# Depthwise convolution in two half-width PSUM accumulators, and sample value products regrouped, in a conformer and attention trunk on one core

## What is computed

```
z = u @ w_in                      # 2048 -> 3 x 2048
a, b, gate = split(z)
c = a * sigmoid(b)
full = concat([history, c])       # 30 earlier positions
y = depthwise_conv(full, conv_w)  # 31 taps per feature
y = silu(layer_norm(y + conv_b))
out = (y * silu(gate)) @ w_out
```

## Time and profile before

| | |
|---|---|
| Median of 3 runs | 3295.57 us (3295.47 to 3299.87) |
| The profiled execution, own time | 3296.47 us |
| Its span | 3294.8 us |
| TensorE busy | 3107.7 us, 94% |
| VectorE busy | 1503.7 us, 46% |
| GpSimd busy | 1551.4 us, 47% |
| ScalarE busy | 850.9 us, 26% |
| Mean granted TensorE clock | 0.972 of full speed |

### The profile page before, as it was taken

How to read it: one execution, slowest core, us unless ns; L and a number is a source line. 1 busy time by engine, 2 the same in 40 slices (tenths; PEclk the granted TensorE clock), 3 DMA queues, 4 the chain that set the end, 5 groups by cost and what they waited for, 6 DMA issues and landing times.

```text
span 3294.8 us, 50429 instructions
## 1 busy us (share of the span) xinstructions
PE 3107.7 (94%) x19117; PEld 2987.6 (91%) x19117; DVE 1503.7 (46%) x1729; ACT 850.9 (26%) x1708; POOL 1551.4 (47%) x1153
## 2 busy tenths in 40 slices
PE   6999999999999999999968999999999999899996
PEld 6999999999889999999948898899899889799995
DVE  6999999999831114000091324333433343500043
ACT  5121211211221224121231223222222222422232
POOL 2778778787733334333343333233233323144475
PEclk9999999999999999999989999999999999899998
DMA  5121221211122225221272211111111211433386
GB/s 162 41 71 50 57 59 47 71 53 53 55 99 92 89 94 168 65 72 65 85 278 94 57 51 46 51 49 43 55 42 51 55 41 48 142 98 93 98 293 225
DMA packets 171678, 284.87 MB, mean 86 GB/s; under 512 B 62009, under 2 KB 72505, under 8 KB 171577
## 3 DMA queue, kind: packets, MB, share of 16 engines
q1 hardware_dynamic: 127328, 222.48, 22.4%
q10 hardware_dynamic: 41912, 52.32, 4.4%
q0 software_dynamic: 2352, 8.88, 0.7%
HBM read 218.44 MB, written 67.15 MB: 87 GB/s over the span
## 4 chain that ended last, share of the span: by engine, by line
PE 47%; POOL 16%; issue 15%; DVE 13%; ACT 4%; DMA 4%; SPq 0%; POOLq 0%; ACTq 0%; DVEq 0%
PE z_even L514 8%; PE z_even L515 8%; PE z_even L517 8%; PE z_odd L514 7%; PE z_odd L515 7%; PE z_odd L517 6%; POOL w_lo L1017 6%; POOL work L1098 3%; POOL work L1090 3%; DMA work<-conv_scratch 2%; ACT work L935 1%; DVE work L1410 1%; DVE work L1413 1%; POOL work L1126 1%; DMA work<-out_scratch 1%
## 5 line engine op out<-in xcount | busy, mean ns | idle before, releaser
L1017 POOL TENSOR_TENSOR w_lo<-w_raw,w_hi 128x512 fp32r<-128x512 f32 x528 | 748.4, 1426 | 1368.6 <-ACT w_hi L734 1368.0
L514 PE MATMUL z_even<-u_hi,w_hi 128*128 128x364 f32 (+1 forms) x2784 | 926.3, 333 | 79.8 <-POOL u_lo L1178 33.6
L514 PE MATMUL z_odd<-u_hi,w_hi 128*128 128x364 f32 (+1 forms) x2784 | 940.8, 338 | 53.5 <-POOL w_lo L1017 53.5
L515 PE MATMUL z_odd<-u_lo,w_hi 128*128 128x364 f32 (+1 forms) x2784 | 925.3, 332 | 0.0
L515 PE MATMUL z_even<-u_lo,w_hi 128*128 128x364 f32 (+1 forms) x2784 | 922.1, 331 | 0.0
L734 ACT ACTIVATE w_hi<-w_raw 128x512 fp32r<-128x512 f32 x528 | 331.5, 630 | 1690.0 <-PE z_even L517 813.8
L517 PE MATMUL z_odd<-u_hi,w_lo 128*128 128x364 f32 (+1 forms) x2784 | 637.8, 330 | 0.0
L517 PE MATMUL z_even<-u_hi,w_lo 128*128 128x364 f32 (+1 forms) x2784 | 635.2, 329 | 0.0
L514 PEld LDWEIGHTS z_even<-u_hi,w_hi 128*128 128x128 f32 x2784 | 530.4, 191 | 98.6 <-issue 27.0
L514 PEld LDWEIGHTS z_odd<-u_hi,w_hi 128*128 128x128 f32 x2784 | 532.8, 191 | 91.9 <-POOL w_lo L1017 49.7
L515 PEld LDWEIGHTS z_odd<-u_lo,w_hi 128*128 128x128 f32 x2784 | 533.7, 192 | 0.1
(11 more groups left out here) (148 smaller groups left out, 2234.6 us busy)
## 6 DMA issues: line engine op xcount, KB each, us to landing
w_raw<-in_w SPq DMA_DIRECT2D x528, 256.0 KB, 2.7
work<-in_x SPq DMA_DIRECT2D x32, 544.0 KB, 5.8
work<-branch_scratch SPq DMA_DIRECT2D x31, 544.0 KB, 5.1
conv_scratch<-work ACTq DMA_DIRECT2D x16, 544.0 KB, 2.7
work<-conv_scratch SPq DMA_DIRECT2D x16, 544.0 KB, 3.8
resid_scratch<-work ACTq DMA_DIRECT2D x16, 544.0 KB, 6.5
branch_scratch<-work ACTq DMA_DIRECT2D x16, 512.0 KB, 2.6
branch_scratch<-work POOLq DMA_DIRECT2D x15, 544.0 KB, 3.0
```

Source lines behind the costliest of these rows:

```text
L514: pe.matmul(o, w_hi[:, q, at:at + P], chunk(u_hi[:, k, :], c), start=(i == 0), stop=False)
L515: pe.matmul(o, w_hi[:, q, at:at + P], chunk(u_lo[:, k, :], c), start=False, stop=False)
L1017: pool.tensor_tensor(w_lo[:, q, :], w_raw[:, q, :], w_hi[:, q, :].bitcast(F32), ALU.subtract).then_inc(w_lo_ready, 1)
```

## The change

The convolution works in two halves of 512 positions, one in each bank of `aux`. For each half VectorE makes tap 0 with the bias itself, by a `tensor_scalar` from `cp` into PSUM, and then taps 1 to 30, the halves in turn; all accumulate in PSUM. Each of them still waits for the instruction two before it, which is now the same half's tap before. ScalarE's tap 0, the row `odd_taps`, the semaphore `tap0_ready` and the final addition are gone. The last taps count up `conv_ready` by two for each group. VectorE may start the next group's tap 0 when ScalarE has copied `aux1` once (`conv_read`), and ScalarE squares its own copy `y_st` instead of reading `aux1` a second time.

In `sample_values` the 16 products with cached values come first, the two head halves p (the upper and lower 64 output partitions) in turn, and then the 16 with new values. Only the first matmul for each p has the start flag, and only the last one the stop flag.

```diff
--- before.py
+++ after.py
@@ -136,8 +136,8 @@
             return out
 
 
-        (r_a, sig, y_st, y_sq, acc_y, acc_y2, cp, cs_flat, ys, prod, odd_taps) = places(
-            T, T, T, T, T, T, TP + 32, SB * SEG, TS, 4 * SS * CW, TP)
+        (r_a, sig, y_st, y_sq, acc_y, acc_y2, cp, cs_flat, ys, prod) = places(
+            T, T, T, T, T, T, TP + 32, SB * SEG, TS, 4 * SS * CW)
         cs = cs_flat.rearrange("p (b s) -> p b s", b=SB)
 
         s_st = [region(8 * T, T), region(9 * T, T), region(T, T), region(3 * T, T)]
@@ -223,7 +223,7 @@
         sig_ready = sem("sig_ready")
         sigr_ready = sem("sigr_ready")
         hist_in = sem("hist_in")
-        tap0_ready = sem("tap0_ready")
+        conv_read = sem("conv_read")
         conv_ready = sem("conv_ready")
         tap = sem("tap")
         ys_ready = sem("ys_ready")
@@ -654,13 +654,18 @@
                 pe.wait_ge(pt_read, 17 * g + 16 + 2)
                 pe.wait_ge(o_read, 9 * g + 7 + 1)
                 pe.sem_inc(pe_passed, 1)
-                for i in range(4):
-                    p, bh = i // 2, i % 2
-                    for r in range(4):
-                        b = 4 * bh + r
-                        o = z_even[HD * p:HD * p + HD, 1, 32 * b:32 * b + 32]
-                        pe.matmul(o, vc[:, b, :], pp[:, i, 32 * r:32 * r + 32], start=True, stop=False)
-                        mm = pe.matmul(o, vn[0:SS, b, :], pc[0:SS, i, 32 * r:32 * r + 32], start=False, stop=True)
+                def out(p, b):
+                    return z_even[HD * p:HD * p + HD, 1, 32 * b:32 * b + 32]
+
+                for b in range(SB):
+                    for p in range(2):
+                        pe.matmul(out(p, b), vc[:, b, :], pp[:, 2 * p + b // 4, 32 * (b % 4):32 * (b % 4) + 32],
+                                  start=(b == 0), stop=False, skip_group_check=True)
+                for b in range(SB):
+                    for p in range(2):
+                        mm = pe.matmul(out(p, b), vn[0:SS, b, :],
+                                       pc[0:SS, 2 * p + b // 4, 32 * (b % 4):32 * (b % 4) + 32],
+                                       start=False, stop=(b == SB - 1), skip_group_check=True)
                 mm.then_inc(pv_done, 1)
 
             def heads(g, jj, samples):
@@ -754,14 +759,15 @@
             def read_conv(j):
 
 
-                act.wait_ge(conv_ready, j + 1)
+                act.wait_ge(conv_ready, 2 * (j + 1))
                 act.wait_ge(ys_ready, j + 1)
                 ge(act, y_added, j)
                 ge(act, y_out, 16 * j)
                 bias = cols[:, bass.ds(C_CB + j, 1)]
-                act.activation(y_st[:, 0:TP], aux1, ACT.Copy)
+                act.activation(y_st[:, 0:TP], aux1, ACT.Copy).then_inc(conv_read, 1)
                 act.activation(y_st[:, TP:T], ys, ACT.Identity, bias=bias)
-                act.activation(y_sq[:, 0:TP], aux1, ACT.Square)
+                act.wait_ge(conv_read, j + 1)
+                act.activation(y_sq[:, 0:TP], y_st[:, 0:TP], ACT.Square)
                 act.activation(y_sq[:, TP:T], ys, ACT.Square, bias=bias).then_inc(y_ready, 1)
                 act.wait_ge(y_ready, j + 1)
                 act.dma_start(y_d[bass.ds(j, 1)].rearrange("o p t -> (o p) t"), y_st).then_inc(y_out, 16)
@@ -775,8 +781,6 @@
                     read_conv(j - 1)
                 split_w(2 * j + 2, 3)
                 act.wait_ge(z_read, 2 * j + 2)
-                act.activation(aux1, cp[:, 0:TP], ACT.Identity, scale=cols[:, bass.ds(C_CW + j * CW, 1)],
-                               bias=cols[:, bass.ds(C_CB + j, 1)]).then_inc(tap0_ready, 1)
                 act.dma_start(scp_t[bass.ds(j, 1)].rearrange("o p s -> (o p) s"), cp[:, TP:TP + HIST]
                               ).then_inc(state_out, 16)
                 act.wait_ge(hist_in, 16 * (j + 1))
@@ -1293,7 +1297,7 @@
                 dve.wait_ge(sigr_ready, j + 1)
                 ge(dve, ys_ready, j)
                 ge(dve, state_out, 32 * j)
-                ge(dve, conv_ready, j)
+                ge(dve, conv_ready, 2 * j)
                 n0, n1 = CHUNKS[0][1], CHUNKS[1][1]
                 dve.tensor_tensor(cp[:, HIST:HIST + n0], z_odd[:, 0, 0:n0], chunk(sig, 0), ALU.mult)
                 dve.tensor_tensor(cp[:, HIST + n0:HIST + n0 + n1], z_odd[:, 1, 0:n1], chunk(sig, 1), ALU.mult)
@@ -1304,20 +1308,23 @@
                                   sig[:, TP:T].rearrange("p (b t) -> p b t", b=SB), ALU.mult).then_inc(z_read, 1)
 
                 dve.wait_ge(z_read, 2 * j + 2)
-                dve.tensor_scalar(odd_taps, cp[:, 1:1 + TP], cols[:, bass.ds(C_CW + j * CW + 1, 1)], None,
-                                  ALU.mult).then_inc(tap, 1)
-                dve.wait_ge(tap0_ready, j + 1)
-                for i in range(2, CW):
-                    if i > 2:
-                        dve.wait_ge(tap, (CW - 1) * j + i - 2)
-                    acc = odd_taps if i % 2 else aux1
-                    dve.scalar_tensor_tensor(out=acc, in0=cp[:, i:i + TP],
-                                             scalar=cols[:, bass.ds(C_CW + j * CW + i, 1)], in1=acc,
-                                             op0=ALU.mult, op1=ALU.add).then_inc(tap, 1)
+                ge(dve, conv_read, j)
+                for h in range(2):
+                    dve.tensor_scalar(aux[:, h, :], cp[:, 512 * h:512 * h + 512],
+                                      cols[:, bass.ds(C_CW + j * CW, 1)], cols[:, bass.ds(C_CB + j, 1)],
+                                      ALU.mult, ALU.add).then_inc(tap, 1)
+                for i in range(1, CW):
+                    for h in range(2):
+                        dve.wait_ge(tap, 2 * (CW - 1) * j + 2 * i + h - 1)
+                        ins = dve.scalar_tensor_tensor(out=aux[:, h, :], in0=cp[:, i + 512 * h:i + 512 * h + 512],
+                                                       scalar=cols[:, bass.ds(C_CW + j * CW + i, 1)],
+                                                       in1=aux[:, h, :], op0=ALU.mult, op1=ALU.add)
+                        if i < CW - 1:
+                            ins.then_inc(tap, 1)
+                        else:
+                            ins.then_inc(conv_ready, 1)
                     if i == CW // 2 and nxt:
                         read_z(2 * j + 2, z_even, sig, r_a)
-                dve.wait_ge(tap, (CW - 1) * j + CW - 1)
-                dve.tensor_tensor(aux1, aux1, odd_taps, ALU.add).then_inc(conv_ready, 1)
 
             glu(0, True)
             with dve.Fori(1, KT - 1) as j:
```

## The result

The changed kernel takes 3223.40 us (median of 4 runs, 3220.35 to 3225.86) against 3297.72 for the kernel before beside it: a ratio of 0.9772, 95% interval 0.9756 to 0.9789. Its profiled execution took 3223.49 us, 73.0 less than the one before. The forecast was 3215, with 81.2 us of gain.

What follows compares the result with a forecast made beforehand. VectorE was taken to bound the GLU stage, TensorE following closely. Gains of 49.0 us there, 9.0 after the last group and 23.2 from the sample products, 81.2 in all, gave 3215 us; range 3202 to 3246.

Steps and rivals of the forecast that it cites:

- The VectorE part: VectorE's convolution in the GLU stage: 62 instructions at a pitch of 0.655 us, a group costing 43.9 us, not 51.34.
- Tap 0, without a row of its own: First instruction of each half on VectorE: given the same pitch as a tap, 0.655 us, between 0.61 and 0.74.
- The bound passes to TensorE: GLU stage: TensorE's pair of tiles needs 47.6 us, more than VectorE's 43.9 a group; all 49.0 us lost are gained.
- Rival (a): GLU stage: VectorE stays the bound, without overlap at a pitch of 0.74 and 49.1 us a group; 3238 us, chance 0.12.
- Rival (d): VectorE's doubled instructions each pay a fixed cost; slower from a pitch of 0.80, at 0.90 3396 us; chance 0.04.
- GpSimd at nothing: GLU stage: GpSimd's `w_lo` for odd tiles comes in time, so GpSimd costs TensorE no wait.
- the 1.3 us of the working: GpSimd in odd tiles: third quarter's `w_lo` done at 34.4 us, needed at 35.7, at durations of the kernel before.
- Rival (c): GLU stage: GpSimd stays late on 15 odd tiles, keeping 45 of the 49 us lost; 3260 us, chance 0.10.
- After the last group: TensorE's wait for the sums after two gate tiles: 49.9 us from the 33rd tile's start, not 58.9; 9.0 less.
- The sample products: TensorE's 64 machine matmuls in `sample_values`: 40 ns each, 2.6 us in place of 8.46; four times 5.8, 23.2 us saved.
- Rival (b): Sample products on TensorE give nothing, a fixed time being paid for each; 3238 us, chance 0.09.
- VectorE's copy, the next tile's wait for it, and the loads of the next group follow the products and move with them: Behind the sample products: what follows moves earlier with them, so the full 5.8 us is saved four times.

Runs made afterwards that it cites:

- quarters: The changed kernel with four PSUM accumulators of 256 in place of two halves, each tap waiting for the one four before it: 3300.18 us, ratio 1.0001.

## Why the prediction was right, and where not

- *The VectorE part.* Right. Pitch 0.655 forecast, 0.658 measured. Tap 0, without a row of its own, lasts 810 ns where a tap lasts 749: 0.06 more, twice a group. "The bound passes to TensorE" is as seen: 48.8 us of the forecast 49.0 came back in the 30 tiles. Rival (a), VectorE as the bound through instructions that don't overlap, is out: starts lie 0.09 us ahead of the end before. The Trainium skill (VectorE: DVE Perf Modes, The DRAIN you can't avoid), from which the prediction took the rule for this rival, adds in the same place that a next instruction that is not held starts earlier. The prediction left that half out; the 0.09 us agree with it. Rival (d), the price of more instructions, wasn't met at 62, but quarters show that it is real: twice their pitch is 0.784, near the 0.80 at which the prediction let the change lose, and they took the time of the kernel before.
- *GpSimd at nothing.* Right, and its margin was larger than the 1.3 us of the working: the sample convolution shrank by 6.5 us. Rival (c) is out.
- *After the last group.* 9.0 forecast, 8.6 measured.
- *The sample products.* 23.2 us forecast, 14.5 measured, with two misses that partly cancel. Rival (b), no gain, is out. The products gave more than forecast: they take 2.2 us where 2.6 were taken, and the 8.46 us before were those of the first group only, where the other three took 9.87, 9.81 and 9.43. In all 28.9 us of products are gone.

  **What failed is the step "VectorE's copy, the next tile's wait for it, and the loads of the next group follow the products and move with them"**: the waits behind them grew by 12.0 us in all. In the three groups with a branch back, the wait was the branch's and not the copy's. It is issued 15 machine matmuls before the products' end, so faster products cover 0.63 us of it in place of 2.75: that is 6.4 us. The branch itself was longer, by 0.55, 1.52 and 1.40 us: 3.5. The sign was there before: the 2.12 us behind the first group's products stand as "issue" in its trace.

  In the fourth group the wait is for the copy, but the copy did not move with the products. VectorE had two instructions for `u_lo` (1.78 us each) and the read of the odd tile in front of it, and it ran at 2773.68, 2.3 us after the products' end; the wait went from 0.52 to 2.78 us.
- From the odd tile's start to the next even tile's the gains are thus 3.6, 4.1, 4.2 and 5.0 us. The fourth group gave 2.4 back in the two tiles behind it, which wait for `u_lo` in both kernels (7.4 us before, 9.3 after). Together 14.5.
- The sum as measured: 48.8 + 8.6 + 14.5 = 71.9 of 73.0 us. Another 0.7 lie ahead of the third tile, whose start varies from 82.8 to 84.5 us among the kernels run here, so they are no gain of the change. The miss of 8 us is the sample term. That it was not larger is luck: the waits and the two tiles behind the fourth group cost 14.4 us that the working put at nothing, and 5.7 of them were made up by the products, mostly because the old ones were longer than the working took them to be.

## To carry to other kernels

A long chain of multiply and add on VectorE beside a busy GpSimd belongs in PSUM: one SBUF input in place of two made taps faster by a third, steadied them, and gave GpSimd a third of its product time back. Splitting the accumulator in two takes out the direct wait, worth 0.12 us a tap here; splitting it further only adds each instruction's own 0.13 us, which ate the whole gain at four. And before shortening the last work ahead of a loop's end, read the branch's own duration and what was covering it: it may be the next thing that is waited for. Here, writing the loop out was worth 20 us, 6 of them by the clock behind the wait.

## What was not expected of the hardware

- TensorE's branch back over the long outer loop takes 3.35 to 5.40 us, that of the inner loops about 0.21. That this is the fetch of instructions from far back would fit, but no run shows it. Nor is it settled why the branch took 3.35 to 4.16 us before and 4.71 to 4.90 after. Its length isn't fixed by the products alone: it was 3.35 to 4.41 with only the convolution changed, and 3.48 to 5.06 with only the products changed.
- A direct wait against a register in front of a VectorE instruction goes with a pitch 0.11 us longer than one against a constant (1.433 and 1.325 at 1024 wide). The two also differ in that one stands in a loop and the other is written out; no run separates these. Where each tap waits for the one two before it, the pitch is 0.658 in either.
